# Stationary tiles interleaved by column and moving operands read backwards in a two-block transformer kernel

## The reference

```
hn = rms_norm(h, ln_pre_mix);  proj = hn @ w_in            # 1024 -> 2312
mix = concat(swa_sink_attention(...), forgetting_attention(...))
h = h + rms_norm(mix @ w_out, ln_post_mix)
gu = rms_norm(h, ln_pre_ffn) @ w_gate_up                    # 1024 -> 2 * 2816
h = h + rms_norm((silu(gu[:F]) * gu[F:]) @ w_down, ln_post_ffn)
```

## Time and profile before

| What | Value |
|---|---|
| runs, median | 1712.26 us |
| profiled execution, first to last instruction | 1708.3 us |
| TensorE matmuls busy | 1687.0 us, 99% |
| weight loads busy | 1401.2 us, 82% |
| VectorE busy | 1065.2 us, 62% |
| ScalarE busy | 723.3 us, 42% |
| GpSimd busy | 154.8 us, 9% |
| moved by DMA | 177.49 MB, mean 104 GB/s |
| mean granted TensorE clock | 0.994 |

### The profile page before, as it was taken

One profiled execution on the slowest core, in us unless ns is written; L12 is line 12 of the kernel. 1 busy time (PEld: TensorE's weight loads), 2 busy tenths in 40 slices (PEclk: granted clock), 3 DMA queues, 4 the chain that ended last, 5 costly groups with the idle time before them and its releaser, 6 DMA issues.

```text
span 1708.3 us, 21445 instructions
## 1 busy us (share of the span) xinstructions
PE 1687.0 (99%) x8588; PEld 1401.2 (82%) x8588; DVE 1065.2 (62%) x1779; ACT 723.3 (42%) x1155; POOL 154.8 (9%) x144
## 2 busy tenths in 40 slices
PE   8999999999999999999999999999999999999997
PEld 8877777888888888888888888889888888888886
DVE  7355557766665347745769665657554769667565
ACT  5436664322222237476423222535566533332533
POOL 2100000000000000111100000011211100000012
PEclk9999999999999999999999999999999999999998
DMA  4331012555554321221222222221322122222221
GB/s 178 116 112 50 26 50 87 201 196 194 197 197 160 111 99 75 99 84 65 75 99 92 97 90 94 96 99 50 124 99 75 49 99 99 97 91 90 93 99 50
DMA packets 31138, 177.49 MB, mean 104 GB/s; under 512 B 3677, under 2 KB 5869, under 8 KB 13886
## 3 DMA queue, kind: packets, MB, share of 16 engines
q1 hardware_dynamic: 22048, 144.71, 23.6%
q0 software_dynamic: 8608, 31.21, 5.3%
q10 hardware_dynamic: 382, 0.19, 0.0%
HBM read 171.28 MB, written 4.78 MB: 103 GB/s over the span
## 4 chain that ended last, share of the span: by engine, by line
PE 96%; DVE 2%; DMA 1%; ACT 1%; issue 0%; ACTq 0%; DVEq 0%
PE ps L640 29%; PE ps L642 29%; PE ps L641 28%; PE ps L1264 1%; PE ps L1252 1%; PE ps L875 1%; PE ps L905 1%; PE ps L838 1%; DVE h L1905 1%; PE ps L1099 1%; PE ps L897 1%; PE ps L678 1%; PE ps L870 0%; PE ps L836 0%; DMA w_raw<-in_w 0%; PE ps L849 0%
## 5 line engine op out<-in xcount | busy, mean ns | idle before, releaser
L640 PE MATMUL ps<-Xh,w_hi 128*128 128x512 f32 (+2 forms) x1760 | 667.0, 379 | 4.7 <-DVE y L1905 2.1
L642 PE MATMUL ps<-Xh,w_lo 128*128 128x512 f32 (+2 forms) x1760 | 655.7, 373 | 0.0
L641 PE MATMUL ps<-Xl,w_hi 128*128 128x512 f32 (+2 forms) x1760 | 655.6, 373 | 0.0
L1905 DVE TENSOR_TENSOR w_lo<-w_raw,w_hi 128x2048 fp32r<-128x2048 f32 (+1 forms) x161 | 312.2, 1940 | 252.1 <-ACT w_hi L1344 251.8
L640 PEld LDWEIGHTS ps<-Xh,w_hi 128*128 128x128 f32 x1760 | 331.8, 189 | 68.9 <-issue 10.8
L1344 ACT ACTIVATE w_hi<-w_raw 128x2048 fp32r<-128x2048 f32 (+1 forms) x158 | 260.5, 1652 | 294.1 <-DMA w_raw<-in_w 271.2
L641 PEld LDWEIGHTS ps<-Xl,w_hi 128*128 128x128 f32 x1760 | 332.0, 189 | 59.1 <-issue 2.6
L642 PEld LDWEIGHTS ps<-Xh,w_lo 128*128 128x128 f32 x1760 | 331.6, 188 | 57.9
L1912 DVE SCALAR_TENSOR_TENSOR cacc<-ain,vec,cacc 128x512 f32<-128x512 f32 x240 | 166.4, 764 | 0.0
L1344 ACT ACTIVATE gt<-ps 128x512 f32<-128x512 f32 x48 | 28.6, 596 | 200.7 <-PE ps L642 200.6
L640 PE MATMUL ps<-act_h,w_hi 128*128 128x512 f32 (+1 forms) x192 | 71.5, 373 | 1.7 <-DVE act_l L1905 1.7
(11 more groups left out here) (322 smaller groups left out, 2165.1 us busy)
## 6 DMA issues: line engine op xcount, KB each, us to landing
w_raw<-in_w SPq DMA_DIRECT2D x134, 1024.0 KB, 4.8
ada_w<-in_w_ada POOLq DMA_DIRECT2D x48, 512.0 KB, 4.7
bias_scratch<-brow POOLq DMA_DIRECT2D x2, 1312.0 KB, 6.6
h<-in_xT SPq DMA_DIRECT2D x4, 512.0 KB, 5.9
out<-h SPq DMA_DIRECT2D x8, 256.0 KB, 2.1
bias<-bias_scratch POOLq DMA_DIRECT2D x1, 1024.0 KB, 9.3
bias<-bias_scratch POOLq DMA_DIRECT2D x1, 512.0 KB, 7.4
cact<-in_c POOLq DMA_DIRECT2D x1, 512.0 KB, 6.5
```

The lines of the kernel that those rows point to most:

```text
L640: nc.tensor.matmul(o_, whi, xhi, start=start, stop=False)
L641: nc.tensor.matmul(o_, whi, xlo, start=False, stop=False)
L642: return nc.tensor.matmul(o_, wlo, xhi, start=False, stop=stop)
L1905: return nc.vector.tensor_tensor(o_, a_, b_, op)
```

## The change

On the host, the two tiles of a pair are interleaved column by column: column 0 of tile 0, column 0 of tile 1, column 1 of tile 0, and so on. Four tiles of a row block become two such interleaved pairs, eight become four. A stationary tile is then read with a step of two float32 (8 bytes) over 1024 bytes. Weights that serve as the moving operand keep their layout. Nothing changes in size, in DMA or in the splitting, which treat a slot as one run of 2048 columns, and a quarter of a slot still holds the same row blocks.

On the chip, `mm3` reverses the free axis of its output and of its two moving operands, so that every matmul in it reads its moving columns from the last to the first and writes its output columns in that order. The stationary operand isn't reversed. Each output column still gets the same sum, in the same place.

```diff
@@ mm3 @@
             def mm3(o_, whi, wlo, xhi, xlo, start, stop):
+                o_, xhi, xlo = o_[:, ::-1], xhi[:, ::-1], xlo[:, ::-1]
                 nc.tensor.matmul(o_, whi, xhi, start=start, stop=False)
                 nc.tensor.matmul(o_, whi, xlo, start=False, stop=False)
                 return nc.tensor.matmul(o_, wlo, xhi, start=False, stop=stop)
@@ w @@
             def w(g, c0, n=P):
-                return w_hi[:, g % NBUF, c0:c0 + n], w_lo[:, g % NBUF, c0:c0 + n]
+
+                if n == P:
+                    first = c0 - c0 % (2 * P) + c0 % (2 * P) // P
+                    c = slice(first, first + 2 * P - 1, 2)
+                else:
+                    c = slice(c0, c0 + n)
+                return w_hi[:, g % NBUF, c], w_lo[:, g % NBUF, c]
@@ host @@
-def _slot(*parts):
-
-    flat = [np.concatenate(tiles, axis=2).reshape(P, -1) for tiles in parts]
+def _between(tiles):
+
+    t = np.concatenate(tiles, axis=2)
+    return t.reshape(P, t.shape[1], -1, 2, P).swapaxes(3, 4).reshape(t.shape)
+
+
+def _slot(stationary, moving=None):
+
+    flat = [_between(stationary).reshape(P, -1)] if stationary else []
+    if moving:
+        flat.append(np.concatenate(moving, axis=2).reshape(P, -1))
     flat = np.concatenate(flat, axis=1)
     return np.pad(flat, ((0, 0), (0, SLOT - flat.shape[1])))
@@ _stream @@
-    def rows4(w_, r0, cols):
-        slots.append(_slot([_tile(w_[r0:r0 + 4 * P], cols)]))
+    def rows4(w_, r0, cols, moving=False):
+        tile = [_tile(w_[r0:r0 + 4 * P], cols)]
+        slots.append(_slot(None, tile) if moving else _slot(tile))
...
-        rows4(w_in, 512 * i, r(vb, 512))
+        rows4(w_in, 512 * i, r(vb, 512), True)
...
-        slots.append(w_down[256 * i:256 * i + 256].reshape(2, P, D).transpose(1, 0, 2).reshape(P, -1))
+        slots.append(_slot([_tile(w_down[256 * i:256 * i + 256], r(0, D))]))
```

## The result

The change made the kernel slower: 1751.76 us, the median of 4 runs between 1749.39 and 1755.05, against 1710.91 us before (four runs, the three above and one more). The ratio is 1.0248 with a 95% interval of 1.0227 to 1.0268. The profiled execution has a span of 1747.6 us, 39.3 us more than the one before.

A forecast was written before the change was run, and what follows sets the result against it. Bound by TensorE's matmul count times the distance between starts. Span 1708.3 - 67.4 + 4 (shorter softmax cover) = 1645 us; the median lies 4.0 us above, so 1649 us, 3.7% faster; range 1630 to 1750.

The forecast's parts named there:

- The bound and what could matter: Whole kernel: matmul count times distance between starts; edits touching neither are worth nothing; TensorE's matmuls busy 99% of the span.
- the part on the stationary step: In mm3, load at 9.9 and backwards moving stream at 9.6 bytes a ns never meet if in phase and starting together.
- the term of 11.0 ns x 6129 = 67.4 us less: In mm3 behind 254 us, 5457 matmuls of 512 columns and 672 of 256 each lose an excess of 11.0 ns.
- the 13.3 ns on top: In mm3, time per matmul beyond its columns, at 512 and 256 columns alike; 2.3 ns remain in float32, 11.0 are excess.
- if both start together: In mm3 in phase, condition for the streams never meeting; otherwise about a third of the gain, up to 1690 us.
- The 16-column loads in the earlier trace: Seven matmuls with 16 stationary columns took 231.4 ns each; called the strongest evidence against the mechanism, for no change at 0.13.
- The unseen accesses taken at nothing: In mm3, the stationary read with a step of two and the backwards read, both without a row, were priced at nothing.
- the bound of 11.0 ns: Stationary step of 8 bytes in mm3: could cost nothing or as much as the excess has now again, 11.0 ns.
- that of 201 ns: Backwards read in mm3: could cost nothing or a second cycle a column, some 201 ns; half-rate rival about 3000 us, 0.07.
- the rhythm is lost: Rival: all mm3 products fall to the out-of-phase pace, 5.5 ns x 6129 = 34 us, 1746 us; chance 0.12.

The follow-up runs named there:

- The backwards kernel: The kernel before with only the line reversing mm3's moving operands and output added, slots and load step as before; 1744.92 us, ratio 1.021.

## Why the prediction was wrong

**The bound and what could matter** were right. The kernel is a count of matmuls times a pace, the counts stayed, no wait took over, and host layout, DMA and splits cost nothing, as the split times and counts show.

**The step that failed** is the argument in the part on the stationary step, and with it the term of 11.0 ns x 6129 = 67.4 us less: that the 13.3 ns on top are cycles which the moving stream loses when it meets the load, and that two streams of one speed in opposite directions "never meet" and shed them. Measured are 6.7 ns more on each of the 5457 wide matmuls, 36 us, and nothing on the 672 narrow ones (120.0 ns before and after). The condition "if both start together" doesn't save it: in the profile of the changed kernel the matmul of L641 and the load for L642 both start at 400.14 us. The argument was built on one true observation, that the pace depends on the phase of the operands, which the kernel before with its operands apart confirms in the block (1.6% slower). The further steps were never in a row. The 16-column loads in the earlier trace rows spoke against them, and I noted that and gave it too little weight: patterns with 16 columns and with one repeated column have since shown that the excess doesn't come from how much the load reads. With the operands apart by 128 bytes, this idea gave the changed kernel 1665 us at most; it took 1741.66.

**The unseen accesses taken at nothing** were the sign error. "I take nothing for both" was priced from the speed of the streams. Either edit alone moves a wide matmul in phase from 544 to 560 cycles, 6.7 ns, inside the bound of 11.0 ns that I had set for the step and far from that of 201 ns for the backwards read. They don't add: 560 cycles is the pace of backwards reads at nearly any distance, with either step. Why, no run shows.

**The rival that came nearest** is the one named "the rhythm is lost", to which I gave 0.12: all products fall to about the out-of-phase pace, 232.2 ns, 1746 us. Measured are 233.3 ns and 1751.76 us. It was short by 1.1 ns for 5457 matmuls, 6 us, and it applied its 5.5 ns to the 672 narrow matmuls, which kept 120.0 ns, 4 us too much. That gives 1748 us; the stretches at 236.7 ns, which it didn't foresee, took the time past the end of the range at 1750. Its nearness in time is in part luck. It needs a stream that no longer goes forwards, and the kernel with the step alone has both forwards and in phase and is as slow.

**The rest of the 39.3 us.** The backwards kernel has a span of 1743.5 us, 35.2 more than before. The changed kernel has 4.1 us on top. The stretches at 236.7 ns account for about that: 1438 of its wide matmuls stand in them, some 3.3 ns each over 233.3, 4.7 us. The timeline shows that what ran just before makes the difference. Of the unbroken stretches of a dozen or more wide `mm3` matmuls, all ten behind the two float32 matmuls of a token sum (L685) go at 236.7 ns, all sixteen behind the ten transposes (L1259) at 233.3 or 233.4, with the same kind of product; of the sixteen that follow narrower score products of the second block, every other one goes at 236.7. A stretch keeps its pace until the next break, or until the weights become the moving operand and the stationary one has step 1 again. The kernel with backwards reads alone passes the same breaks and stays at 233.3 or 233.4 behind both; so does the changed kernel with its operands apart (233.3 to 233.8), and with the step alone nothing behind them is above 233.4. The pattern of the changed kernel alone on the core has no such break before it. Patterns at other distances do hold this pace from the start (backwards at 8 and 240 bytes, 11.36 us, 236.7 ns). Why this break, with this pair of edits, brings it on stays open.

**What stays open** is why 544 cycles and not fewer. The excess depends on the distance of the streams, on the direction and step of the reads, on what ran before, and unevenly on the width, but it doesn't shrink with a shorter load. Matmuls without any load beside them, which would separate the streams for good, weren't tried. The Trainium skill (TensorE: Matmul & The Clock Gate, Step-by-step: what each phase is for) says that the load of the next tile doesn't steal read bandwidth from the running matmul. That agrees with the 16-column load, which gains nothing. It doesn't cover that moving the stationary data by 64 bytes changes the pace from 226.7 to 233.3 ns.

## What to carry to other kernels

Where the pace of equal matmuls is the bound, read operands forwards, with step 1 and in the same place modulo 256 bytes: of some 80 patterns of this shape none was clearly faster. A mechanism inferred from one dependence needs its second test before it may price an edit, and the row that contradicts it (here the small load) should have set the chance. Patterns put alone on the core, with a single short run each, gave the block's main paces within 0.3 ns. They missed the one that depends on what ran before, so the block itself has the last word.

## What the runs showed of the hardware

- Reduced-type matmuls with a fresh 128-column load: 544 cycles for 512 columns forwards in phase, 560 in phase when backwards or with a load step of 8 bytes; 288 cycles for 256 columns in all of these except backwards with step 1, 284 (5.68 us for 48).
- The pace can depend on what ran before: the same products go at 233.3 or 236.7 ns in the changed kernel, behind transposes or behind a float32 sum; and turning the direction every two matmuls costs as much as all backwards (11.19 us for 48), turning it every matmul half as much (11.05 us).
- The direction of the output write costs nothing (10.89 us for 48 either way), nor does a plain float32 matmul feel the direction of its moving read (41.20 us for 96 both ways).
- A load lasts 188 ns with a step of 4 bytes, 193 with 8, 309 with 16; with the moving stream backwards and a step of 8 it lasts 197.
